# A two-layer block on one core: the first stage's modulation vectors in units of 256 shift and 256 scale columns, the first two projections in quarters of k-tiles, x in four transfers

## The reference, cut to what matters

```
mod(c)   = silu(c) @ w_mod + b_mod          # 1024 -> 6 * 1024; one row for x, one for the context
shift, scale = mod[0:1024], mod[1024:2048]  # the first two of the six
h        = rms_norm(tokens) * gain * (1 + scale) + shift     # 256 context + 256 latent tokens
p        = h @ w_in                         # q, k, v of the delta branch come first: 3 * 1024 columns
qkv      = silu(depthwise_conv(p[:, :3072]))
gates, decays                               # from 64 further columns of w_in
mod[2048:6144]                              # gates and shift/scale for the later layers
```

## Time and profile before

| | us |
|---|---|
| median of 3 runs | 2003.64 (2002.41 to 2004.31) |
| the profiled execution, its own time | 2004.77 |
| its span | 2003.0 |

### The profile page before, as it was taken

One profiled execution on the slowest core, in us unless ns is written; L12 is line 12 of the kernel. 1 busy time (PEld: TensorE's weight loads), 2 busy tenths in 40 slices (PEclk: granted clock), 3 DMA queues, 4 the chain that ended last, 5 costly groups with the idle time before them and its releaser, 6 DMA issues.

```text
span 2003.0 us, 23794 instructions
## 1 busy us (share of the span) xinstructions
PE 1856.7 (93%) x9223; PEld 1031.3 (51%) x9223; DVE 669.7 (33%) x1443; ACT 408.1 (20%) x824; POOL 67.5 (3%) x103
## 2 busy tenths in 40 slices
PE   6999999998999899999799999798999799999997
PEld 3446456887887443333332333333333255777775
DVE  1988466347622211222121121121021214432223
ACT  3223630336221110111100010110010023520011
POOL 1000500100000000000000000000000000000000
PEclk9999999899999899999999999999999999999999
DMA  9714447325384999999999999999999942124442
GB/s 392 276 66 152 153 131 195 113 76 164 126 319 198 370 429 428 427 428 427 427 428 427 427 428 427 427 427 428 428 427 428 384 165 97 64 85 157 157 157 94
DMA packets 98609, 568.84 MB, mean 284 GB/s; under 512 B 33104, under 2 KB 43216, under 8 KB 67408
## 3 DMA queue, kind: packets, MB, share of 16 engines
q1 hardware_dynamic: 92192, 561.93, 69.9%
q10 hardware_dynamic: 6320, 5.51, 1.0%
HBM read 555.55 MB, written 11.67 MB: 283 GB/s over the span
## 4 chain that ended last, share of the span: by engine, by line
PE 42%; DMA 17%; issue 3%; DVE 3%; ACT 1%; DVEq 0%; SPq 0%
DMA expert_ring<-in_w_gu_units 13%; PE close_bank L2251 11%; PE close_bank L2306 8%; PE close_bank L2667 7%; DMA tail<-in_w_gu_units 4%; PE close_bank L2677 4%; PE close_bank L2222 3%; PE close_bank L2494 3%; PE close_bank L2604 1%; DVE ob L2132 1%; PE close_bank L2589 1%; PE close_bank L2658 1%; DVE lr L2112 1%; PE close_bank L2293 0%; DVE hT L2140 0%
## 5 line engine op out<-in xcount | busy, mean ns | idle before, releaser
L2251 PE MATMUL close_bank<-expert_ring,hT 128*64 128x512 f32 x1248 | 279.1, 594 | 26.1 <-DMA expert_ring<-in_w_gu_units 26.1
L2251 PEld LDWEIGHTS close_bank<-expert_ring,hT 128*64 128x64 f32 x1248 | 87.0, 137 | 205.0 <-issue 152.8
L2139 DVE TENSOR_SCALAR hT<-close_bank 128x512 f32<-128x512 f32 x32 | 22.1, 692 | 447.2 <-PE close_bank L2251 447.2
L2193 ACT ACTIVATE hT<-hT 128x512 f32<-128x512 f32 x32 | 20.1, 630 | 681.8 <-DVE hT L2139 681.8
L500 PE MATMUL mix_in_pj<-hT,mix_in_pj_ring 128*128 128x512 f32 (+1 forms) x384 | 140.8, 527 | 3.8 <-DVE hT L632 2.7
L2667 PE MATMUL close_bank<-hT,expert_ring 128*128 128x256 f32 x640 | 141.4, 379 | 0.0
L2667 PEld LDWEIGHTS close_bank<-hT,expert_ring 128*128 128x128 f32 x640 | 121.6, 190 | 25.1 <-issue 9.6
L2306 PE MATMUL close_bank<-expert_ring,hT 128*64 128x512 f32 x304 | 134.1, 592 | 0.0
L2306 PE MATMUL close_bank<-expert_ring,h2T 128*64 128x512 f32 x304 | 134.1, 592 | 0.0
L154 PE MATMUL delta_scan_fill_bank<-hT,fill_w 128*128 128x512 f32 (+1 forms) x320 | 112.2, 510 | 5.5 <-PEq L81 2.8
L500 PEld LDWEIGHTS mix_in_pj<-hT,mix_in_pj_ring 128*128 128x128 f32 x384 | 73.1, 192 | 69.2 <-issue 62.7
(11 more groups left out here) (501 smaller groups left out, 2613.5 us busy)
## 6 DMA issues: line engine op xcount, KB each, us to landing
expert_ring<-in_w_gu_units SPq DMA_DIRECT2D x78, 2048.0 KB, 38.3
expert_ring<-in_w_down_units SPq DMA_DIRECT2D x38, 2048.0 KB, 38.9
ahead<-in_w_gu_units SPq DMA_DIRECT2D x13, 2048.0 KB, 40.9
tail<-in_w_gu_units SPq DMA_DIRECT2D x13, 2048.0 KB, 39.1
late<-in_w_gu_units SPq DMA_DIRECT2D x12, 2048.0 KB, 37.0
pool<-in_w_gu_units SPq DMA_DIRECT2D x12, 2048.0 KB, 37.9
mix_in_wm<-in_w_mod_units SPq DMA_DIRECT2D x11, 2048.0 KB, 12.4
expert_ring<-in_w_up_units SPq DMA_DIRECT2D x22, 1024.0 KB, 5.5
```

What stands on the lines that cost most here:

```text
L2139: v.tensor_scalar(glu, gb[j], LIMIT, None, ALU.min).then_inc(s_glu, 1)
L2251: m = pe.matmul(b[halves[h], :], xT[:, k, x], unit[z][:, r0 + c0 + 512 * h:r0 + c0 + 512 * h + 512], start=False, stop=(k == KT - 1))
```

## The change

A modulation unit of the first four now holds 256 shift columns and the 256 scale columns that go with them, so that unit n serves k-tiles 2n and 2n + 1 alone. The layout of `w_mod` in DRAM is permuted on the host for it. PE does the transposes first, then for each unit the product, the columns, and the quarter of projections 0 and 1 that it allows. ACT and DVE follow in four quarters. x comes in four transfers with a semaphore each, the small tables are issued before u0, and u2 goes behind ring unit 1. ACT runs a root on one element before the squares. The two memsets of DVE at the start change places. Counts waited for on `s_col` follow from one increment per unit.

```
# SP
-                sp.dma_start(xc, A.xall.rearrange("t p d -> p t d")).then_inc(s_x, 16)
-                leading(0)
+                for t in (2, 3, 0, 1):
+                    sp.dma_start(xc[:, t, :], A.xall[t]).then_inc(s_x[t], 16)
                 for dst, src in ((C.const, A.consts), (bcol, A.b_mod_col), ...
-                leading(2)
+                leading(0)
                 unit(0)
                 leading(1)
                 unit(1)
+                leading(2)
                 leading(3)
# ACT
                 act.activation(ccolp[:, :, 0:2], ccol[:], ACT.Silu).then_inc(s_c, 1)
-                act.wait_ge(s_x, 16)
+                act.activation(warm[:], C.eps[:], ACT.Sqrt)
                 for n, t in enumerate((2, 3, 0, 1)):
+                    act.wait_ge(s_x[t], 16)
                     act.activation(junk, xc[:, t, :], ACT.Square, ...
...
-                mod_row(0)
                 for t in (2, 3, 0, 1):
                     turned(t)
-                mod_row(2)
                 act.wait_ge(s_xt, 2 * NTILE)
-                for half in range(2):
-                    act.wait_ge(s_ab, 4 * half + 4)
-                    for k in range(4 * half, 4 * half + 4):
+                for n in range(HEAD):
+                    mod_row(n)
+                    act.wait_ge(s_ab, 4 * n + 4)
+                    for k in (2 * n, 2 * n + 1):
                         act.activation(S.hT[:, k, 0:L], ...
-                    if half == 0:
-                        mod_row(1)
-                        mod_row(3)
# PE
+                quarter = lambda n: range(2 * n, 2 * n + 2)
                 pe.wait_ge(s_c, 1)
-                mod_unit(0)
                 pe.wait_ge(s_const, 80)
                 for t in (2, 3, 0, 1):
                     turn(t)
-                mod_unit(2)
-                columns([0, 2], 0)
+                mod_unit(0)
+                columns(0)
                 pe.wait_ge(s_pw[0], 16)
-                project_part(0, range(KT // 2))
-                mod_unit(1)
-                pe.wait_ge(s_pw[1], 16)
-                project_part(1, range(KT // 2), (0,))
-                mod_unit(3)
-                columns([1], 0)
-                project_part(1, range(KT // 2), (1,))
-                columns([3], 0)
-                for n in range(2):
-                    project_part(n, range(KT // 2, KT)).then_inc(s_pf[n], 1)
+                project_part(0, quarter(0))
+                for n in range(1, HEAD):
+                    mod_unit(n)
+                    if n == 1:
+                        pe.wait_ge(s_pw[1], 16)
+                    project_part(1, quarter(n - 1))
+                    columns(n)
+                    i = project_part(0, quarter(n))
+                i.then_inc(s_pf[0], 1)
+                project_part(1, quarter(HEAD - 1)).then_inc(s_pf[1], 1)
                 project(2)
# DVE
-                for half in range(2):
-                    ks = slice(4 * half, 4 * half + 4)
-                    v.wait_ge(s_col, 2 * half + 1)
+                for n in range(HEAD):
+                    ks = slice(2 * n, 2 * n + 2)
+                    v.wait_ge(s_col, n + 1)
                     # the same two additions, two products and one step per k-tile, for ks
# host
-        "w_mod_units": f(x["w_mod"][0].reshape(KT, P, -1, 512).transpose(2, 1, 0, 3)),
+        "w_mod_units": f(np.concatenate([x["w_mod"][0][:, :2 * D].reshape(D, 2, 4, 256).transpose(0, 2, 1, 3).reshape(D, 2 * D),
+                                         x["w_mod"][0][:, 2 * D:]], axis=1).reshape(KT, P, -1, 512).transpose(2, 1, 0, 3)),
```

More of the change, by code:

```diff
@@ L224, in mix_in_stage @@
         pc, small = s.ps("pc", [P, 512]), s.ps("small", [P, 512])
+        warm = s.sb("warm", [P, 1])
         s_cc, s_c, s_z, s_const, s_x, s_gb, s_w, s_w2 = (s.sem("cond_in"), s.sem("cond_silu"), s.sem("cond_zero"), s.sem("tables_in"),
-                                                         s.sem("x_in"), s.sem("gate_bias_in"), s.sems("mod_first_in", HEAD),
+                                                         s.sems("x_in", NTILE), s.sem("gate_bias_in"), s.sems("mod_first_in", HEAD),
                                                          s.sems("mod_later_in", HEAD - 1))
@@ L236, in mix_in_stage @@
         s_md = s.sem("mod_products")
-        USES = ["u0", "u2", "u1", "u3", "b4", "b5", "q0", "q1", "u10", "u11", "b10", "b11"]
+        USES = ["u0", "u1", "u2", "u3", "b4", "b5", "q0", "q1", "u10", "u11", "b10", "b11"]
         TURN = {k: (i % 2, i // 2) for i, k in enumerate(USES)}
@@ L356, in mod_row @@
                     if n >= VEC[1]:
-                        act.wait_ge(s_col, 4)
+                        act.wait_ge(s_col, HEAD + 1)
                     act.activation(modrow[:, n % 4, :], b[:], ACT.Copy).then_inc(s_free[TURN[f"u{n}"][0]], 1)
@@ L380, in _ @@
                 act.wait_ge(s_cc, 16)
-                act.wait_ge(s_z, 1)
+                act.wait_ge(s_z, 2)
                 act.activation(ccolp[:, :, 0:2], ccol[:], ACT.Silu).then_inc(s_c, 1)
-                act.wait_ge(s_x, 16)
+                act.activation(warm[:], C.eps[:], ACT.Sqrt)
                 for n, t in enumerate((2, 3, 0, 1)):
+                    act.wait_ge(s_x[t], 16)
                     act.activation(junk, xc[:, t, :], ACT.Square, accum_out=ss[:, t:t + 1]).then_inc(s_ss, 1)
@@ L457, in mod_unit, with columns @@
                     i.then_inc(s_full[TURN[f"u{n}"][0]], 1)
[L459 to L464, removed]
+                def columns(n):
+                    copied_pm(pe, f"u{n}")
+                    for j in range(4):
+                        c = KT * (j // 2) + 2 * n + j % 2
+                        i = pe.matmul(pc[:, 2 * c:2 * c + 2], modrow[:, n % 4, j * P:(j + 1) * P], sel[:], start=True, stop=True)
                     i.then_inc(s_col, 1)
@@ L604, in convolve @@
                     assert done["taps"] == TAPS_DONE[n]
+                v.memset(C.eps[:], EPS).then_inc(s_z, 1)
                 v.memset(ccolp[:], 0.0).then_inc(s_z, 1)
-                v.memset(C.eps[:], EPS)
                 v.wait_ge(s_const, 80)
@@ L623, in _ @@
                                         deep(bcol[:, c], 2), ALU.add).then_inc(s_ab, 1)
-                    v.wait_ge(s_ab, 4 * half + 2)
+                    v.wait_ge(s_ab, 4 * n + 2)
                     for q in range(2):
@@ L627, in _ @@
                                                ALU.add, ALU.mult).then_inc(s_ab, 1)
-                    v.wait_ge(s_ab, 4 * half + 4)
-                    if half == 0:
+                    v.wait_ge(s_ab, 4 * n + 4)
+                    if n == 0:
                         v.wait_ge(s_xt, 2 * NTILE)
@@ L640, in mod_products @@
                             see_pm(v, spread_out[n])
-                    v.wait_ge(s_col, 3)
+                    v.wait_ge(s_col, HEAD)
                     count = PAIR_DONE[u0] - 2 * KT
@@ L729, in _ @@
                 convolve(10)
-                v.wait_ge(s_col, 4)
+                v.wait_ge(s_col, HEAD + 1)
                 link(v.tensor_tensor(mcol2[:], pc[:, 0:4 * KT].rearrange("p (k t) -> p k t", t=2),
```

## The result

| | us |
|---|---|
| changed kernel, median of 6 runs | 2012.52 (2009.86 to 2014.03) |
| kernel before, median of 6 runs beside them | 2004.03 (2002.41 to 2007.10) |
| ratio | 1.0035, 95% interval 1.0025 to 1.0045 |
| profiled execution of the changed kernel | 2012.83, span 2011.0 |

The change makes the kernel slower by 0.35%, 7.0 us by the ratio. The forecast was slower by 4.3 us, with the range's upper end at 2012.3: by the ratio on the median it started from (2003.64) the time is 2010.7, inside the range; the raw median of the six runs, 2012.52, stands 0.2 us above it.

What follows compares the result with a forecast made beforehand. TensorE's list of work was taken to bound the first stage. The terms -4.8 + 5.5 + 1.8 + 1.9 gave +4.4 us (+4.3 as good), so 2007.9 us on the median of 2003.64; range 2003.0 to 2012.3.

Steps and rivals of the forecast that it cites:

- What bounds the stage: First stage from 27.03 us: TensorE's list of work binds, not transfers; a shift after projection 1 moves the end one for one.
- Start of the transposes: Head of the kernel: transposes start at 12.0 us instead of 18.23, a gain of 6.2 us.
- the rival of the second table: Head: the root's table does not hold the square, so a second load returns: +1.9 us, 2009.8; chance 0.06.
- Transposes and the clock: Head: transposes, now TensorE's first work, meet the slow clock, lose 1.7 us (bounds 0 and 3.6) and end at 17.3.
- The rival that they do not wake the clock: Head: all 32 transposes and the first modulation unit run at 1.2 GHz: 2011.6 us; chance 0.11.
- From there to E: Transposes' end to projection 1's end: first projection at 22.2 us instead of 27.03, then 42.1 us, 5.5 more than before.
- E: Time at which projections 0 and 1 are done: 63.6 us before, forecast 64.3, or 66.1 with one further clock fall.
- The 42.1 of the sum: First projection to E: 32 products, three units, three columns with a wait, one first clock loss of 1.8 us.
- Further falls: Between the quarters: TensorE's clock falls once in three stretches of 2.28 us, costing 1.8 us (ends 0 and 5.5).
- Ring unit 2: Before projection 2: TensorE newly waits 1.9 us for this unit's transfer (bounds 0.9 and 4).
- What else moves: After the quarters: DVE reaches `mod_products(4)` at 59.2 us, 8.9 late, with room for 13.0; no one waits for it meanwhile.
- a sign of being wrong: At the stage's end: it moves by another amount than E and the new ring wait together.

Runs made afterwards that it cites:

- e9: Kernel before with only the change's new head, and GpSimd's split of the biases held back until projection 0 is done: ratio 0.9997 to the kernel before.
- e4: Kernel before with only the change's head (x in four transfers, tables ahead of u0, early table load, transposes first): ratio 0.9979 to the kernel before.
- e8: Kernel before (halves kept) with the change's head, late GpSimd bias split, and part of projection 1 moved behind both pairs of columns: ratio 0.9982.
- the covered kernel: Changed kernel with half of each later quarter of projection 1 moved behind the columns, beside DVE's step: ratio 0.9991 to the kernel before.
- e2: Changed kernel with two idle products of 256 columns behind the columns of each of the three later rounds: ratio 1.0014 to the kernel before.
- e5: The changed kernel again, unaltered, timed beside other runs: ratio 1.0036 to the kernel before.
- e10: Changed kernel with GpSimd kept busy from the start by 32 unneeded subtractions of 128x768: ratio 1.0078 to the kernel before (4 runs).
- e11: As e8, plus 7 idle products on zeros from about 2 us and two idle products in the first wait for DVE: ratio 0.9966, median 1998.63 us.
- e1: Same run as the covered kernel: changed kernel with half of each later quarter of projection 1 behind the columns; ratio 0.9991 to the kernel before.
- e3: Changed kernel with ring unit 2 loaded early into a buffer of its own: ratio 1.0014 to the kernel before.
- e6: Changed kernel with the old head put back (x in one transfer, u0 ahead of the tables, modulation unit 0 first, no early table load): ratio 1.0038.
- e7: Changed kernel with half-quarters behind the columns, ring unit 2 in its own buffer, and GpSimd's bias split held back until projection 0 is done: ratio 0.9978.

## Why the prediction was right, point by point

**What bounds the stage.** Right. Projection 0 began 4.8 us earlier and the end came later, as a list of work on one engine does when more is put into it. No other engine took over: DVE's wait for ACT's exponentials stayed 5.7 us. The two runs that split the change put the loss in the quarters.

**Start of the transposes.** 12.0 us was forecast, 11.83 measured; they ended at 17.17 for 17.3. The early table load worked and no further load appeared, so the rival of the second table falls.

**Transposes and the clock.** The forecast's 1.7 us of loss were 5.34 - 3.62 = 1.7. That it fits to a tenth is luck: in the changed kernel's second profile the loss was 2.8 us, within the bounds of 0 and 3.6. The rival that they do not wake the clock is false: the first 17 of them fill 12.0 to 15.3 us, the other 15 run in 1.8 us, and the first modulation unit behind them took 1.92 us, the fast time. The run with the early idle products has the record itself: 0.50, then 1.00 with transposes alone. The Trainium skill ("TensorE: Matmul & The Clock Gate", Part 4: PE-mode transpose) says that transposes do not count as busy for the clock. By that rule the first projection would have come 3.7 us later, as the rival has it. Here the measurement decides against it.

**From there to E.** The first projection came at 22.24 for 22.2. From there to projection 1's end were 45.8 us, from 22.24 to 68.0 (61.09 and 8 products of 0.863 us). The 42.1 of the sum hold one fall, the one behind the start; with the two more that this profile had (2 x 1.7) it is 45.5. The four waits of 1.31 us stand as forecast.

**Further falls.** This is the term of the sum that was too small: one fall in three stretches was taken, there were two in the first profile, at 35.9 and 49.5 us, one in the second, and 7 in 12 stretches over the four profiles that have them. The one stretch of 47.53 to 49.81 in the kernel before, at the fast pace behind it, was read as if a stretch of this kind held two times in three; it was one draw of a thing that varies from run to run. The stretch of 3.3 us ahead of the first projection was read as certain to make it fall, and is a draw too: in the halved kernels with the early head the clock fell behind it in one profile (e9) and not in two (e4, e8).

**Ring unit 2.** Forecast 1.9 us, measured 1.44 and 1.46 (2.31 in the covered kernel), within the bounds of 0.9 and 4. The mechanism is right: the wait went when the unit had its own buffer.

**What else moves.** DVE's `mod_products(4)` began at 61.00 us, 10.6 late, and its wait of 3.0 us was used up, as said. (Both waits in the earlier trace rows are for ACT; the prediction has one for PE, which changes nothing.) Not seen was the longer fall at 189.5 us, 1.6 us for the stage's end. By it the stage's end moved by more than E and the new wait together, which the prediction had named as a sign of being wrong. This fall is a draw as well: it is as long as here in three other profiles (e2, e5, e10), 3.4 us in e4, e9 and e11, and absent in e1, e3, e6, e7 and e8.

In all: +0.7 at E as forecast, 3.4 for two further falls and 0.3 of small things make 4.4 at E; 1.4 of ring wait and its start-up make the 6.0 us at projection 2; 1.6 from the late fall, less 0.5 from the shorter ring wait ahead of it, make 7.1 at the stage's end. The forecast had 4.3 of it: 1.8 where the falls took 3.4, nothing for the late one, and 0.5 too much for the ring. The mechanism was right: TensorE's list, waits made twice as often, a transfer no longer hidden. The size was not, 4.3 us for 7.0; the range held it because its upper end allowed for further falls. That the change is slower at all was given 0.49 against 0.45 for no difference, hardly a decision; the measured 7.0 us is clear of the noise.

## What to carry to other kernels

Where one engine's list is the bound, an earlier start is worth only what the list does not take back: count each hand-over that is made twice as often, and put independent work behind each producer so that the round trip through the other engines is covered. Short stretches with little work on TensorE cost twice, once as idle time and once, in some runs, as a slower clock behind them; read them as a chance per stretch and not from the one that the trace at hand shows. When a piece that hid a transfer is cut in half, ask whether the transfer still fits.

## What the hardware showed unexpectedly

A subtraction of 128x768 on GpSimd (1.80 us) holds DVE's instructions up: two products of two columns took 1.88 us instead of 0.23, and with GpSimd subtracting without a break DVE's scaling of four 128x1024 tiles took 7.01 us instead of 2.74. Not all are hit: the additions that read PSUM kept their 0.23 us in that run, beside products of 0.91 to 1.28 us.

Transposes alone raised TensorE's clock (0.50 to 15.5 us, 1.00 from 15.7 on in e11), and 2.4 us without work between 9.7 and 12.1 us were enough to lose it there. Products on zeros raise it too: their pace went from 0.85 to 0.43 us an instruction. Column products of two columns do not reliably hold it, though TensorE is busy without a gap in them: the clock fell to 0.50 behind 3.6 us of them in the kernel before, at 185.1 us, and in five of the other profiles it did not fall there.
